# Moving two of six modulation blocks from TensorE to VectorE in a two-block float32 transformer kernel

## The reference, cut to what matters

```python
def ada_modulation(cond, w, b):
    m = jax.nn.silu(cond) @ w + b           # [2048] @ [2048, 6*2048]
    return jnp.split(m[..., None, :], N_MOD, axis=-1)
...
sh_a, sc_a, g_a, sh_m, sc_m, g_m = ada_modulation(c, w_ada[layer], b_ada[layer])
csh_a, csc_a, cg_a, csh_m, csc_m, cg_m = ada_modulation(c_ctx, w_ada[layer], b_ada[layer])
h = modulate(rms_norm_2(x, norm_attn_w[layer]), sh_a, sc_a)
hc = modulate(rms_norm_2(ctx, norm_attn_w[layer]), csh_a, csc_a)
...
x = x + g_a * (jnp.concatenate([attn, pool], axis=-1) @ w_out[layer])
hm = modulate(rms_norm_2(x, norm_mlp_w[layer]), sh_m, sc_m)
x = x + g_m * squared_relu_mlp(hm, w_mlp_up[layer], w_mlp_down[layer])
```

## Time and profile before

| what | value |
|---|---|
| time, median of 3 runs | 1827.35 us (1827.26 to 1829.85) |
| the profiled execution, its own time | 1827.91 us |
| its span, first to last instruction | 1826.3 us |
| TensorE matmul busy | 1668.9 us, 91% of the span |
| VectorE busy | 1049.8 us, 57% |
| ScalarE busy | 759.0 us, 42% |
| GpSimd busy | 31.5 us, 2% |
| mean granted TensorE clock | 0.969 of 2.4 GHz |
| moved by DMA | 374.71 MB, mean 205 GB/s |

### The profile page before, as it was taken

One profiled execution on the slowest core, in us unless ns is written; L12 is line 12 of the kernel. 1 busy time (PEld: TensorE's weight loads), 2 busy tenths in 40 slices (PEclk: granted clock), 3 DMA queues, 4 the chain that ended last, 5 costly groups with the idle time before them and its releaser, 6 DMA issues.

```text
span 1826.3 us, 35299 instructions
## 1 busy us (share of the span) xinstructions
PE 1668.9 (91%) x12462; PEld 1506.7 (83%) x12462; DVE 1049.8 (57%) x1568; ACT 759.0 (42%) x1068; POOL 31.5 (2%) x48
## 2 busy tenths in 40 slices
PE   3899999899978977988889959999999999999996
PEld 2788888788867867866779949989998999899985
DVE  4445454455556557466665575655565555555675
ACT  5344444343433334434434435434543454345442
POOL 0000000000000000000000000000000000000000
PEclk9999999899998998999999969999999999999998
DMA  7677777687875774654235525555555555555552
GB/s 308 242 270 258 268 266 264 217 300 290 300 253 201 286 285 135 219 196 160 94 127 155 179 69 182 185 184 184 182 185 186 184 182 186 187 180 183 185 192 94
DMA packets 88370, 374.71 MB, mean 205 GB/s; under 512 B 10256, under 2 KB 10768, under 8 KB 75488
## 3 DMA queue, kind: packets, MB, share of 16 engines
q1 hardware_dynamic: 87120, 369.54, 59.3%
q0 software_dynamic: 1168, 4.00, 0.7%
HBM read 371.40 MB, written 2.10 MB: 205 GB/s over the span
## 4 chain that ended last, share of the span: by engine, by line
issue 73%; PE 12%; DVE 9%; ACT 3%; DMA 1%; DVEq 0%; POOL 0%; ACTq 0%; POOLq 0%; SPq 0%
PE G L389 3%; PE G L390 3%; PE G L391 3%; DVE lo L1034 3%; ACT hi L711 1%; DVE sm L1328 1%; DMA ada_raw<-w_ada_dram 1%; PE M L609 1%; DVE blk L1034 1%; DVE blk L1341 1%; ACT blk L952 1%; PE ADA L430 1%; PE S L660 1%; PE S L583 1%; DVE blk L1349 0%
## 5 line engine op out<-in xcount | busy, mean ns | idle before, releaser
L1034 DVE TENSOR_TENSOR lo<-raw,hi 128x1024 fp32r<-128x1024 f32 x496 | 607.5, 1225 | 425.9 <-ACT hi L711 392.7
L389 PE MATMUL G<-actA,hi 128*128 128x256 f32 x2368 | 690.7, 292 | 32.1 <-DVE actA L1034 31.5
L711 ACT ACTIVATE hi<-raw 128x1024 fp32r<-128x1024 f32 x496 | 525.6, 1060 | 369.7 <-PE G L416 194.7
L390 PE MATMUL G<-actA,lo 128*128 128x256 f32 x2368 | 675.4, 285 | 0.0
L391 PE MATMUL G<-actA,hi 128*128 128x256 f32 x2368 | 675.0, 285 | 0.0
L389 PEld LDWEIGHTS G<-actA,hi 128*128 128x128 f32 x2368 | 457.5, 193 | 89.7 <-issue 71.2
L390 PEld LDWEIGHTS G<-actA,lo 128*128 128x128 f32 x2368 | 458.2, 194 | 0.3
L391 PEld LDWEIGHTS G<-actA,hi 128*128 128x128 f32 x2368 | 457.8, 193 | 0.0
L415 PE MATMUL G<-actB,hi 128*128 128x512 f32 x1024 | 358.6, 395 | 0.0
L416 PE MATMUL G<-actB,lo 128*128 128x256 f32 x1024 | 287.2, 280 | 0.0
L415 PEld LDWEIGHTS G<-actB,hi 128*128 128x128 f32 x1024 | 192.0, 187 | 44.9
(11 more groups left out here) (167 smaller groups left out, 979.7 us busy)
## 6 DMA issues: line engine op xcount, KB each, us to landing
raw<-stream_dram SPq DMA_DIRECT2D x496, 512.0 KB, 4.2
ada_raw<-w_ada_dram SPq DMA_DIRECT2D x96, 1024.0 KB, 7.0
x_tok<-x_tok_dram SPq DMA_DIRECT2D x1, 2048.0 KB, 8.3
resid<-xT_dram SPq DMA_DIRECT2D x1, 2048.0 KB, 10.9
ctx_tok<-ctx_tok_dram SPq DMA_DIRECT2D x1, 2048.0 KB, 18.0
W<-ctxT_dram POOLq DMA_DIRECT2D x16, 128.0 KB, 6.5
out_dram<-resid SPq DMA_DIRECT2D x4, 512.0 KB, 2.6
ada_raw<-pool_w_dram POOLq DMA_DIRECT2D x1, 1024.0 KB, 5.5
```

Source lines behind the costliest of these rows:

```text
L389: pe.matmul(bank, hi[:, slot, cols], x[:, k, 0:T], start=(k == 0), stop=False, skip_group_check=True)
L390: pe.matmul(bank, lo[:, slot, cols], x[:, k, 0:T], start=False, stop=False, skip_group_check=True)
L711: return act.activation(dst, src, ACT.Copy)
L1034: return dve.tensor_tensor(dst, a, b, op)
```

## The change

Blocks 2 and 3 (32 of the 96 rows) leave TensorE. Slot 1 of `ada_raw` becomes the buffer of these rows during units 0 to 63; ScalarE issues their loads (`part_load`), twice in each group of four units, each when VectorE has used the row before it. VectorE takes a row with four operations of 128x512 (`part_take`): the row's weights times one column of silu(c), added up in the new buffer `part`, four rows (one quarter of a block) at a time. After each fourth row TensorE adds the 128 partitions of `part` with four matmuls of one column (`part_sums`) and VectorE adds the bias (`part_add`). TensorE's own rows of blocks 0 and 1 now stand in units 0 and 2 of each group, none in units 1 and 3, and use slot 0 alone. Block 4 is added in units 64 to 79 and block 5 in the query stage as before. The turn of block 1 now stands in unit 64, and that of block 4 moves from inside unit 80 to behind unit 82. The loops of the head and convolution stages on ScalarE and VectorE, and those of SyncE's modulation loads, are written out.

```diff
+        part = sb("part", [P, 512])
+        PART = S[0][:, 3 * P:3 * P + 4]
...
@@ sync
             for n in range(RING, 2 * RING):
                 weight(n % RING, n)
-            ada(0, 0, first=True)
-            ada(1, 1, first=True)
-            with sp.Fori(0, U_KV // 4) as i:
-                for j in range(4):
-                    ada(i * 4 + j + 2, j % 2)
-                    weight(2 * j % RING, i * 8 + 2 * j + 8)
-                    weight((2 * j + 1) % RING, i * 8 + 2 * j + 9)
+            ada_load(0, 0)
+            for u in range(U_KV):
+                n = u // 2 + 1
+                if u < U_OUT1 - 2 and u % 2 == 0:
+                    ada_load(n, 0, ada_used, n)
+                elif u == U_OUT1 - 2:
+                    ada_load(4 * KT, 0, ada_used, 2 * KT)
+                elif u == U_OUT1 - 1:
+                    ada_load(4 * KT + 1, 1, ada_taken, 2 * KT)
+                elif U_OUT1 <= u < U_KV - 2:
+                    e = u - U_OUT1 + 2
+                    ada_load(4 * KT + e, e % 2, ada_used, 2 * KT + e - 1)
+                weight(2 * u % RING, 2 * u + 8)
+                weight((2 * u + 1) % RING, 2 * u + 9)
...
@@ tensor
+            def part_sums(n):
+                pe.wait_ge(ada_taken, 4 * (n + 1))
+                if n:
+                    pe.wait_ge(part_added, n)
+                for m in range(4):
+                    x = pe.matmul(PART[:, m:m + 1], part[:, m * P:(m + 1) * P], ones[:, 0:1], start=(m == 0), stop=(m == 3),
+                                  skip_group_check=True)
+                x.then_inc(part_summed, 1)
...
             def conv_body(h):
                 at, tail = At(4 * h), h == HEADS
-                unit(at, 0, actA, ada=4 * h)
+                unit(at, 0, actA, ada=2 * h)
...
-                unit(at, 1, actA, ada=4 * h + 1)
+                unit(at, 1, actA)
...
+                if h % 2 == 0:
+                    part_sums(h // 2 - 1)
-                unit(at, 2, actA, ada=4 * h + 2)
+                unit(at, 2, actA, ada=2 * h + 1)
...
-                unit(at, 3, actA, ada=4 * h + 3)
+                unit(at, 3, actA)
...
             for n in range(UNITS_OUT):
-                unit(At(U_OUT1), n, actB, inB, ada=U_OUT1 + n)
+                unit(At(U_OUT1), n, actB, inB, ada=2 * KT + n)
+                if n == 1:
+                    part_sums(7)
...
             at = At(U_KV)
-            half_unit(at, 0, 0, actC, inC)
-            ada_turn()
-            half_unit(at, 0, 1, actC, inC)
+            unit(at, 0, actC, inC)
             total_sums(1)
             half_unit(at, 1, 0, actC)
             broadcast()
             half_unit(at, 1, 1, actC)
             unit(at, 2, actC)
+            ada_turn()
             unit(at, 3, actC)
...
@@ scalar
+            def part_load(n, row):
+                act.wait_ge(ada_taken, n)
+                src = t_in["w_ada"][row] if isinstance(row, int) else t_in["w_ada"][bass.ds(row, 1)].rearrange("a p n -> (a p) n")
+                act.dma_start(ada_raw[:, 1].rearrange("p k n -> p (k n)"), src).then_inc(ada_full[1], 16)
...
             def conv_body(n, tail, i, block=None):
                 split(at, 0, 0)
+                part_load(2 * n, 2 * KT + 2 * n)
...
                 split(at, 3, 0)
+                part_load(2 * n + 1, 2 * KT + 2 * n + 1)
                 act.wait_ge(z_used, turn.value("z_exp"))
                 evacuate(at, 3, yz)
...
@@ vector
+            def part_take(n):
+                if n % 4 == 0 and n:
+                    dve.wait_ge(part_summed, n // 4)
+                dve.wait_ge(ada_full[1], 16 * (n + 1))
+                k = n % 4 * 4
+                for m in range(4):
+                    w, c = ada_raw[:, 1, m, :], cpad[:, k + m, 6:7]
+                    if k + m == 0:
+                        seq(dve.tensor_scalar(part[:], w, c, None, ALU.mult))
+                    elif m < 3:
+                        seq(dve.scalar_tensor_tensor(part[:], w, c, part[:], ALU.mult, ALU.add))
+                    else:
+                        dve.scalar_tensor_tensor(part[:], w, c, part[:], ALU.mult, ALU.add).then_inc(ada_taken, 1)
+                        own(ada_taken)
+            def part_add(n):
+                dve.wait_ge(part_summed, n + 1)
+                at = 2 * KT + 4 * n
+                tt(adav[:, 0, at:at + 4], PART, col("b_ada", at, 4), ALU.add).then_inc(part_added, 1)
+                own(part_added)
...
             def conv_body(j):
                 split(at, 1)
+                if n % 2 == 0:
+                    part_add(n // 2 - 1)
+                part_take(2 * n)
                 split(at, 2, 0)
...
                 silu(z_conv[:, one(j)])
...
                 take_sums(ss[:, 6:8], SUMS[:, 0:2])
+                if j < CONV_TILES - 1:
+                    part_take(2 * n + 1)
...
+            def modulation_ready():
+                ada_add(1, 1)
+                for r in range(2):
+                    dve.scalar_tensor_tensor(scale_a[:, r], adav[:, r, SC_A:SC_A + KT], 1.0, col("norm_attn", 0, KT), ALU.add,
+                                             ALU.mult).then_inc(scale_ready, 1)
+                    own(scale_ready)
+            part_take(2 * KT - 1)
```

More of the change, by code:

```diff
@@ L252, in weight @@
                 sp.dma_start(raw[:, slot, :], src).then_inc(raw_full[slot], 16)
[L254 to L261, removed]
             sp.dma_start(x_tok[:], t_in["x_tok"]).then_inc(tok_in, 16)
@@ L427, in ada_rows @@
                     pe.wait_ge(ada_added, block)
-                pe.wait_ge(ada_full[n % 2], 16 * (n // 2 + 1))
+                slot, load = (0, n + 1) if n < 2 * KT else (n % 2, 2 * KT + (n - 2 * KT) // 2 + 1)
+                pe.wait_ge(ada_full[slot], 16 * load)
                 for g in range(4):
-                    m = pe.matmul(ADA[32 * g:32 * g + 32, :], cpad[:, 4 * (k % 4) + g, 6 - 2 * (k // 4):38 - 2 * (k // 4)], ada_raw[:, n % 2, g, :],
+                    m = pe.matmul(ADA[32 * g:32 * g + 32, :], cpad[:, 4 * (k % 4) + g, 6 - 2 * (k // 4):38 - 2 * (k // 4)], ada_raw[:, slot, g, :],
                                   start=(k == 0), stop=(k == KT - 1), tile_position=(0, 32 * g), skip_group_check=True)
@@ L485, in head_body @@
                 at, prev = At(4 * h), h > 0
-                unit(at, 0, actA, None if prev else inA, ada=4 * h)
+                unit(at, 0, actA, None if prev else inA, ada=2 * h)
                 if prev:
                     head_scores()
-                unit(at, 1, actA, ada=4 * h + 1)
+                unit(at, 1, actA)
                 if prev:
                     head_turn()
-                unit(at, 2, actA, ada=4 * h + 2)
+                if prev and h % 2 == 0:
+                    part_sums(h // 2 - 1)
+                unit(at, 2, actA, ada=2 * h + 1)
                 if prev:
@@ L860, in _ @@
                 act.wait_ge(act_seq, turn.next("seq"))
-            head_body(At(0), None)
-            with turn.lap(act, 3, "act heads") as i:
-                head_body(At(4, 4, i), y_attn[:, bass.ds(i, 1)])
-            head_body(At(16), y_attn[:, 3:4], 0)
-            with turn.lap(act, 3, "act heads") as i:
-                head_body(At(20, 4, i), y_attn[:, bass.ds(i + 4, 1)])
-            conv_body(At(32), True, None, 1)
-            with turn.lap(act, 3, "act conv") as i:
-                conv_body(At(36, 4, i), False, i)
-            conv_body(At(48), False, 3, 2)
-            with turn.lap(act, 3, "act conv") as i:
-                conv_body(At(52, 4, i), False, i + 4)
+            act.dma_start(ada_raw[:, 1].rearrange("p k n -> p (k n)"), t_in["w_ada"][2 * KT]).then_inc(ada_full[1], 16)
+            head_body(0, None)
+            for n in range(1, HEADS):
+                head_body(n, y_attn[:, n - 1:n])
+            conv_body(8, True, None, 0)
+            for n in range(9, 16):
+                conv_body(n, False, n - 9)
+            ada_copy(1)
             high(actB[:, 7, 0:T], t4[:, 1])
@@ L1162, in attn_tile, with conv_body @@
                 own(nt_ready)
-            def conv_body(at, tail, j, i, block=None):
+            def conv_body(j):
+                at, tail, i = At(4 * HEADS + 4 * j), j == 0, j - 1 if j else None
+                n = HEADS + j
                 split(at, 0, 0)
-                if block is not None:
-                    ada_add(block)
                 if tail:
+                    ada_add(0, 0)
                     head_max()
@@ L1274, in out_lap @@
                     split(at, j, 0)
-                    if j == 0 and block is not None:
-                        ada_add(block)
+                    if j == 0 and first:
+                        modulation_ready()
+                    if j == 2 and first:
+                        part_add(7)
                     tt(resid[:, u], resid[:, u], summed(at, j), ALU.add).then_inc(evac_done, 1)
```

105 lines of the change are left out of this document (48 added, 57 removed).

## The result

| | before | after |
|---|---|---|
| median | 1828.6 us (4 runs, 1827.26 to 1829.90) | 1814.36 us (4 runs, 1813.35 to 1815.71) |
| the profiled execution, and its span | 1827.91, 1826.3 us | 1813.97, 1812.3 us |

The ratio is 0.9921, with a 95% interval of 0.9906 to 0.9936: 14.2 us faster, a small change but clear of the noise. The forecast was 1797.5 (a gain of 29.8), with 1811 as its far end. The sign is right, and half of the gain is missing.

A forecast was written before the change was run, and what follows sets the result against it. TensorE was taken to bound the kernel between seams; -38.1 - 1.9 + 7.6 + 1 + 3.5 + 1.5 - 3.4 = -29.8 us took the profiled 1827.91 to 1798.1, or 1797.5 as median, range 1790 to 1811.

The forecast's parts named there:

- Rows off TensorE: Head and convolution groups: 32 rows at 1.19 us leave TensorE, -38.1 us; the new partition sums cost +7.6.
- VectorE's rows: Head and convolution groups: 0.75 us per 512-column operation, 3.2 a row; fits beside TensorE at 85% busy, costing nothing.
- The loads: Modulation loads into the single slot 1 buffer, mainly in convolution groups: +1 us taken, bounds 0 and 18.
- the prediction's formula: Convolution groups: one single-buffer loop takes 2L + 11.5 us, L being load landing time; at 7.4 it equals TensorE's 26.3.
- late-load rival: Convolution groups: the single buffer sets the pace because loads land late; 1807 to 1815 us, chance 0.20.
- Seam after head 0: VectorE's chain to the context broadcast, awaited 6.85 us by TensorE, gets row 1 in it: +3.5 us.
- Seam at unit 64: Row behind `modulation_ready` -1.6 us, half-clock work +2, load of unit 65's row +0 to +4; sum +1.5.
- Seam at unit 80: Without block 4's turn inside unit 80, the sums and VectorE's chain to unit 84's inputs come earlier: -3.4 us.
- The query stage keeps its rows and their waits: 0.: Query stage, adding block 5: its rows and their waits stay as before, 0 us.

The follow-up runs named there:

- e7: The e5 kernel with six VectorE operations instead of four for each of the 32 rows; 1810.68 us, 0.9894 of the kernel before.
- e4: The changed kernel with VectorE's row 1 taken behind the context norm's mean square and diagonal instead of ahead of them; 1813.40 us, 0.9918 of before.
- e6: The e5 kernel with the addition of block 1 and the scales moved ahead of VectorE's row 31 and the split of unit 64; 1796.78 us.
- e1: The changed kernel with SyncE's load order around the query stage put back as before the change; 1804.09 us, 0.9857 of the kernel before.
- e2: The kernel before the change, with only SyncE's load order around the query stage made that of the changed kernel; 1849.49 us, 1.011 of before.
- e3: The changed kernel with the addition of block 0 moved on VectorE ahead of modulation row 15; 1807.06 us, 0.988 of the kernel before.
- e5: The changed kernel with the edits of e1, e3 and e4 together; 1794.28 us, 0.9806 of the kernel before.

## Why the prediction was right in direction and short in size

**Rows off TensorE: right.** A group without sums lasts 25.84 us (378.73 to 404.57) and one with them 26.72 (to 431.29), as worked out from 28.20 in the earlier trace rows and 1.19 in the earlier trace rows: 28.20 - 2 x 1.19 = 25.82, and 0.88 for the sums where 0.95 was taken. The record's 1.06 us would have given 26.08.

**VectorE's rows: right.** 752 ns for 512 columns, where 0.75 was taken between two forms of the earlier trace rows. VectorE is at 83% in the convolution window, and TensorE never waits there; e7 shows that the cover was real and nearly used up.

**The loads: right.** Modulation loads land in 6.3 us at the median on ScalarE's queue and 6.7 over both in 364 to 530 us:

```profile
DMA to landing us min/median/max: 5.0/6.7/8.4
```

That is under the 7.4 at which, by the prediction's formula, the single buffer would set the pace, and under the 7.5 of the earlier trace rows, at 313 GB/s where it was 299. (The 7.4 itself is not shown: e7 has one landing in the loop where the formula has two.) The late-load rival fell, and the +1 was not needed. That the measured 1814.36 lies in that rival's span, 1807 to 1815, is coincidence: the time was lost at other places and by other loads. The Trainium skill (DMA: Bandwidth & Descriptors, "Issuing engines are not separate DMA queues") says that loads started by scalar and sync share the 16 engines, so that ScalarE's loads have no path of their own. Nothing here speaks against it (the share rose only from 0.85 to 0.86 and the stage was not slowed); the loss that it pointed to did not come. The loss that did come needs no bandwidth at all: it is the order of waits within one issuing queue.

**Seam after head 0: right.** The wait grew from 6.85 to 10.47, 3.6 us where 3.5 was taken; e4 takes it away.

**Seam at unit 64: right.** The row came 1.6 us closer to the broadcast ahead of it (gains of 24.5 at the broadcast, 544.20 before and 519.70 after, and of 26.1 at the row), as -1.6 said. Then the next row stands 6.71 us behind (544.41) instead of 4.05, 2.7 lost where +2 was taken for work at half clock: the row's record is 1.93 us, not 1.07. The wait for the load of unit 65 was covered, as e6 shows by uncovering it.

**Seam at unit 80: nearly right.** The gain is 22.6 us at the third row of the stage (574.84 before, 552.23 after) and 26.1 at the sums, 3.5 more. VectorE takes them 25.8 earlier than before, but its first operation behind the broadcast comes only 25.1 earlier: it waits 1.83 us for TensorE there, where it waited 0.87. So 0.7 of the 3.4 did not arrive, and the moved turn itself hid, since VectorE's chain from that operation to the inputs of unit 84 lasts 27.8 us in both kernels.

**The step that failed** is the last of the list: "The query stage keeps its rows and their waits: 0." It measured +9.9. The rows are kept; their waits are not. The prediction followed what moved on TensorE, VectorE and ScalarE; of SyncE it looked at the loads of the stages before, the load of unit 65 above all. The diff shows the written-out loop ending with `u < U_KV - 2`; two rows that the old loop had issued ahead of the stage are missing from it. That was to be seen from the diff and the queue's timeline. e1 and e2 show it from both sides.

**A seam that was not listed**: the addition of block 0 in unit 32, now behind `part_take(15)`. It has no term in the sum and cost 3.9 to 4.5 us at its place, by e3. The prediction looked at what VectorE's row delays after head 0 and at unit 64, and not at the third place, where the turn of a block is answered by VectorE.

**The sum** at unit 84, where neither the query stage nor what follows has its part: 29.8 was forecast and 25.1 came. 4.7 are missing, and 5.7 with the 1 that the loads did not cost. 3.9 to 4.5 of them are unit 32. Half a microsecond is a longer wait for `ss` in the first convolution group (7.70 us after, 7.24 before), 0.7 the part of the moved turn that did not arrive. What is left, some tenths, is too small to be placed. With both misses mended (e3 and e1) and the known seam of head 0 as well, e5 stands at 0.9806, which on the median before of 1827.35 is 1792. The forecast without its +1 and +3.5 would have been 1793. The terms that were priced were priced well; what failed was the list.

One slip stands in the prediction's range. Its bounds of the three seams, added to the forecast, reach from 1793.5 to 1806.7, and 1792.5 without the loads' 1; "1792 to 1803" is too short at its upper end. The stated range of 1790 to 1811 holds both.

Behind the query stage the change loses 1.2 us more (929.5 us from the last turned tile to the end before, 930.6 after). No step of the change touches that part. 1.0 of it is longer busy time of the same 6252 matmul records (877.98 us before, 878.95 after); why they ran slower stays open.

## What to carry to other kernels

When a loop that issues loads is written out or re-cut, list for every stage which loads are in flight at its start, before and after, and compare the lists: a missing pair costs nothing where it is dropped and shows up stages later. When work is put on an engine, list all that other engines wait for from it, seams first; each such answer goes ahead of the new work. And a table of the starts of the same instruction in both traces finds both faults without a theory.

## What was not expected of the hardware

The same work ran under different granted clocks in different kernels. The windows over the same part of the program (about 40 us behind the last turned tile), and the group in it that follows a wait, in e1:

```profile
910.00:920.00 10.00, 7.78 (x46) 7.18 (x45) 8.56 (x16) 3.01 (x5) 0.00 (x0) 0.83 0.43 122
...
914.66 2.57 PE L675 MATMUL S<-blk,ada_raw 128*128 128x256 f32 x8 [2.22 <-DVE blk L1055]
```

and in the change:

```profile
921.00:931.00 10.00, 7.78 (x58) 7.37 (x58) 7.87 (x14) 3.33 (x5) 0.00 (x0) 1.00 0.43 148
...
924.04 1.99 PE L675 MATMUL S<-blk,ada_raw 128*128 128x256 f32 x8 [2.22 <-DVE blk L1055]
```

The wait ahead of the group is the same, 2.22 us, and the busy time too, but the clock is 0.83 in one and 1.00 in the other: in e1 the group's eight records take 2.57 us instead of 1.99, and the 10 us hold 46 matmul records where the change has 58. e1 takes 933.4 us from its last turned tile to the end where the change takes 930.6, and 2.3 of these 2.7 us are busy time of the same 6252 records. So the clock, at places where TensorE works in short pieces, moves the time by a few microseconds that belong to no edit. Terms under about 3 us can be read here from the trace of their own place only.
